# Branch outputs of the hybrid mixer: chunks in pairs on TensorE, six block sums on GpSimd

## The reference, cut to what matters

```
g = sigmoid(gates.reshape(b, s, 3, 1024))
merged = g[:, :, 0] * (o_fox @ w_fox_out) + g[:, :, 1] * (o_dsa @ w_dsa_out) + g[:, :, 2] * (o_sb @ w_sb_out)
return merged @ w_out
```

## Time and profile before

| what | value |
|---|---|
| runs | 2165.32, 2165.68, 2166.57 us; median 2165.68 |
| the profiled execution | 2165.68 us, its span 2163.6 us (2.1 us lie around the span) |
| TensorE busy | 2153.1 us of the span |
| VectorE, ScalarE, GpSimd busy | 1507.8, 597.0, 459.0 us |
| branch stage, first layer | 420.46 to 451.28 us from the span's start |
| branch stage, second layer | 1156.53 to 1187.34 us |

### The profile page before, as it was taken

The page is one execution under the profiler, slowest core; times in us unless marked ns, Lnnn a source line. Parts: engine busy times, 40 slices in busy tenths (PEclk is TensorE's granted clock), DMA queues, the critical chain, the costliest instruction groups (busy, mean ns, idle before and its releaser), DMA issues.

```text
span 2163.6 us, 44071 instructions
## 1 busy us (share of the span) xinstructions
PE 2153.1 (100%) x17524; PEld 2071.0 (96%) x17524; DVE 1507.8 (70%) x3184; ACT 597.0 (28%) x1608; POOL 459.0 (21%) x652
## 2 busy tenths in 40 slices
PE   9999999999999999999999999999999999999998
PEld 8999999899999999999998999999989999889998
DVE  6774856787776677668477777665758774768775
ACT  2210233512221022004433222201425520434530
POOL 1110003600222022100153002211214431313440
PEclk9999999999999999999999999999999999999999
DMA  9556654443664566456544545555636646637653
GB/s 256 164 163 181 165 141 127 137 144 118 188 168 156 169 171 171 162 166 166 148 118 124 169 132 163 164 178 143 181 99 174 174 156 168 175 98 180 163 164 109
DMA packets 571605, 340.40 MB, mean 157 GB/s; under 512 B 45332, under 2 KB 567432, under 8 KB 571400
## 3 DMA queue, kind: packets, MB, share of 16 engines
q1 hardware_dynamic: 566736, 335.46, 55.0%
q10 hardware_dynamic: 4392, 1.08, 0.2%
q0 software_dynamic: 272, 1.05, 0.1%
HBM read 336.49 MB, written 1.05 MB: 156 GB/s over the span
## 4 chain that ended last, share of the span: by engine, by line
PE 85%; issue 8%; POOLq 3%; POOL 2%; DVE 1%; DVEq 0%; ACT 0%; ACTq 0%
PE bank L1105 40%; PE bank L1183 15%; PE bank L719 8%; PE bank L788 4%; PE bank L728 3%; PE bank L905 3%; PE bank L1381 2%; PE bank L1348 1%; PE bank L1341 1%; PE bank L1055 1%; POOLq L2308 1%; POOL arena L2310 1%; PE bank L1230 1%; PE bank L1530 1%; POOLq L2326 1%
## 5 line engine op out<-in xcount | busy, mean ns | idle before, releaser
L1105 PE MATMUL bank<-work,arena 128*128 128x128 f32 x3096 | 387.9, 275 | 0.0
L1105 PEld LDWEIGHTS bank<-work,arena 128*128 128x128 f32 x3096 | 366.4, 192 | 0.0
L2403 DVE TENSOR_TENSOR arena<-ring 128x512 f32<-128x512 f32 (+1 forms) x424 | 282.3, 706 | 93.0 <-PE bank L1183 77.7
L1183 PE MATMUL bank<-gates,arena 128*128 128x128 f32 x1584 | 216.1, 275 | 0.0
L1183 PEld LDWEIGHTS bank<-gates,arena 128*128 128x128 f32 x1584 | 196.2, 192 | 0.0
L1105 PE MATMUL bank<-hT,ring 128*128 128x128 f32 x1392 | 183.9, 275 | 0.0
L1105 PEld LDWEIGHTS bank<-hT,ring 128*128 128x128 f32 x1392 | 169.6, 192 | 0.5 <-DVE work L2403 0.2
L1105 PE MATMUL bank<-work,ring 128*128 128x128 f32 x1264 | 166.3, 275 | 0.0
L2169 POOL TENSOR_TENSOR small<-small 128x2 f32<-128x2 f32 x17 | 13.4, 789 | 707.4 <-DVE small L2400 685.1
L2403 DVE TENSOR_TENSOR arena<-arena,ring 128x512 f32<-128x512 f32 (+1 forms) x212 | 146.8, 692 | 19.6
L1737 ACT ACTIVATE hT<-xT 128x512 f32<-128x512 f32 x48 | 30.1, 629 | 466.2 <-DVE xT L2406 440.4
(11 more groups left out here) (485 smaller groups left out, 3973.0 us busy)
## 6 DMA issues: line engine op xcount, KB each, us to landing
ring<-in_ffn_w_gu SPq DMA_DIRECT2D x174, 512.0 KB, 5.2
ring<-in_w_in SPq DMA_DIRECT2D x126, 512.0 KB, 5.1
ring<-in_ffn_w_down SPq DMA_DIRECT2D x112, 512.0 KB, 4.5
ring<-in_ffn_w_up SPq DMA_DIRECT2D x84, 512.0 KB, 5.3
ring<-in_w_out SPq DMA_DIRECT2D x16, 1024.0 KB, 5.1
ring<-in_ca_w_kv SPq DMA_DIRECT2D x8, 1024.0 KB, 5.2
ring<-in_ffn_w_down SPq DMA_DIRECT2D x24, 256.0 KB, 2.9
ring<-in_w_in SPq DMA_DIRECT2D x20, 256.0 KB, 4.1
```

Of the source, the lines that this page charges most:

```text
L1105: mm = pe.matmul(out_, a[:, c, :], b_[:, c, :], start=(start and c == 0), stop=(c == 3), skip_group_check=True)
L1183: mm = pe.matmul(bank[4 * half + where_][:, S * part + P * m:S * part + P * (m + 1)], stat[name][:, k, P * m:P * (m + 1)], moving, start=( ...
L2403: return v.tensor_tensor(out_, a, b, op)
```

## The change

TensorE takes the chunks in tiles (0, 1), (2, 3), (4, 5), (6), (7): the fox products of the tile's chunks, their dsa and sb products over 128 rows, then all of the tile's products over 64 rows. VectorE gates the fox banks of a tile first (into `a4` rows 0 and 3), then dsa and sb and the adds chunk by chunk. The block sums of chunks 0 to 5 move to GpSimd, which does them in a new function ahead of `memory_sums`. VectorE waits for all six of them before t2 of chunk 6; TensorE waits for four before s1 t1 and for all six before s2 t2.

```diff
+        POOL_TURNS = 6
+        BRANCH_TILES = ((0, 1), (2, 3), (4, 5), (6,), (7,))
...
-                for m in range(C):
-                    if m % 2 == 0:
+                for ms_ in BRANCH_TILES:
+                    if ms_[0] % 2 == 0:
                         view, loaded = slots.next(10)
...
+                    for m in ms_:
+                        b = free("proj_done")
+                        for k in range(3):
+                            mm = pe.matmul(b[:, 0:S], view[:, m % 2, k, :], oT[:, k, :], start=(k == 0), stop=(k == 2))
+                        mm.then_inc(sem["proj_done"], 1)
+                    if ms_[0] == 0:
                         pe.wait_ge(sem["dve_released"], outputs_kept)
...
+                    half_rows = []
+                    for m in ms_:
+                        for own, p0 in (((3, 4), 0), ((5, 6), HD)):
+                            b = free("proj_done")
+                            for k in own:
+                                pe.matmul(b[:, 0:S], view[:, m % 2, k, :], oT[:, k, :], start=(k == own[0]), stop=False)
+                            half_rows.append((b, m, p0))
+                    for b, m, p0 in half_rows:
+                        pe.matmul(b[:, 0:S], view[p0:p0 + HD, m % 2, 7, :], oT[p0:p0 + HD, 7, :], start=False, stop=True)\
                           .then_inc(sem["proj_done"], 1)
...
+                        if q == 0 and out_ is rc and snap == 0:
+                            pe.wait_ge(sem["chunk_turned"], turned - 2)
+                        if q == 0 and snap == 1:
+                            pe.wait_ge(sem["chunk_turned"], turned)
...
+            def branches_turned():
+
+                for m in range(POOL_TURNS):
+                    pool.wait_ge(sem["chunk_merged"], n("chunk_merged"))
+                    t1, t2, t3, t4 = (t_[:, m % 4, :] for t_ in merged_t)
+                    if m < 4:
+                        pool.tensor_tensor(t1, hsT[:, m, P:S], hsT[:, m, 0:P], ALU.subtract)\
+                            .then_inc(sem["chunk_turned"], 1)
+                        continue
+                    pool.drain()
+                    pool.tensor_tensor(t2, hsT[:, m, P:S], t1, ALU.subtract)
+                    pool.tensor_tensor(t3, hsT[:, m, P:S], hsT[:, m - 4, P:S], ALU.subtract)
+                    pool.drain()
+                    pool.tensor_tensor(t4, hsT[:, m, 0:P], t2, ALU.subtract).then_inc(sem["chunk_turned"], 1)
...
+                branches_turned()
                 memory_sums()
...
+                def merge(m, fox):
+                    v.drain()
+                    tt(a4[:, 1, :], fox, a4[:, 1, :], ALU.add)
+                    v.drain()
+                    tt(hsT[:, m, :], a4[:, 1, :], a4[:, 2, :], ALU.add).then_inc(sem["operand_ready"], 1)
+                    if m < POOL_TURNS:
+                        v.drain().then_inc(sem["chunk_merged"], 1)
                     else:
+                        v.drain()
+                        if m == POOL_TURNS:
+                            v.wait_ge(sem["chunk_turned"], n("chunk_turned", POOL_TURNS))
...
                     if m in (2, 4):
                         make_sums()
+
+                def gated(k, m, dst):
+                    v.wait_ge(sem["proj_done"], n("proj_done"))
+                    tt(dst, gates[:, C * k + m, :], seen("dve", "proj_done")[:, 0:S], ALU.mult)\
+                        .then_inc(sem["dve_released"], 1)
+
+                for ms_ in BRANCH_TILES:
+                    for m in ms_:
+                        gated(0, m, (a4[:, 0, :], a4[:, 3, :])[m - ms_[0]])
+                    for m in ms_:
+                        for k in (1, 2):
+                            gated(k, m, a4[:, k, :])
+                        merge(m, (a4[:, 0, :], a4[:, 3, :])[m - ms_[0]])
```

More of the change, by code:

```diff
@@ L347, in build @@
                "pair_turned", "pair_sums", "pair_done", "pair_copied", "pair_added", "z_ready", "hidden_made",
-               "pairs_kept", "scores_kept", "gate_turned", "gate_sums", "gate_paired", "gate_kept", "gate_kept_v", "gate_added",
+               "chunk_merged", "chunk_turned", "pairs_kept", "scores_kept", "gate_turned", "gate_sums", "gate_paired", "gate_kept", "gate_kept_v", "gate_added",
                "gates_ready",
@@ L1337, in attention1 @@
                         pe.wait_ge(*loaded)
[L1338 to L1343, removed]
-                        pe.wait_ge(sem["dve_released"], outputs_kept)
[L1345 to L1350, removed]
+                    for m in ms_:
[4 more added lines that the diff above has]
+                    if ms_[0] == 0:
+                        pe.wait_ge(sem["dve_released"], outputs_kept)
+                    half_rows = []
[7 more added lines that the diff above has]
+                        pe.matmul(b[:, 0:S], view[p0:p0 + HD, m % 2, 7, :], oT[p0:p0 + HD, 7, :], start=False, stop=True)\
                           .then_inc(sem["proj_done"], 1)
@@ L1356, in attention1 @@
                 branches_read = banks.released()
+                turned = n("chunk_turned", POOL_TURNS)
                 for q in range(4):
@@ L3084, in mixer1 @@
                 v.wait_ge(sem["gates_ready"], n("gates_ready"))
[L3085 to L3089, removed]
+                def merge(m, fox):
                     v.drain()
-                    tt(a4[:, 0, :], a4[:, 0, :], a4[:, 1, :], ALU.add)
+                    tt(a4[:, 1, :], fox, a4[:, 1, :], ALU.add)
                     v.drain()
[L3093 to L3097, removed]
-                    else:
+                    tt(hsT[:, m, :], a4[:, 1, :], a4[:, 2, :], ALU.add).then_inc(sem["operand_ready"], 1)
+                    if m < POOL_TURNS:
+                        v.drain().then_inc(sem["chunk_merged"], 1)
+                    else:
+                        v.drain()
+                        if m == POOL_TURNS:
+                            v.wait_ge(sem["chunk_turned"], n("chunk_turned", POOL_TURNS))
+                        t1, t2, t3, t4 = (t_[:, m % 4, :] for t_ in merged_t)
                         ins = tt(t2, hsT[:, m, P:S], t1, ALU.subtract)
```

## The result

Six runs of the changed kernel have a median of 2173.9 us (2173.4 to 2177.1), six of the kernel before on the same chip 2166.1: a ratio of 1.0039, 95% interval 1.0029 to 1.005, so 7.8 us slower. The profiled execution took 2173.69 us, its span is 2171.5 (before: 2163.6).

A forecast was written before the change was run, and what follows sets the result against it. TensorE was taken as the bound, 0.06 us ahead of VectorE. Per layer 0.35 (chain) + 3.0 (`memory_sums` collision) + 0.6 (chunk sums) = 3.95 us; two layers 7.9, so 2165.7 + 7.9 = 2173.6 us, range 2165.8 to 2178.6.

The forecast's parts named there:

- The bound and its margin: Branch stage: TensorE bounds the kernel, with a margin of 0.06 us over VectorE at t2 of chunk 7.
- The switch: TensorE's branch stage: five stretches of half-height work instead of eight save 1.2 us a layer, 2.4 in all.
- rival (c): t2 of chunk 7 comes early enough that TensorE keeps its 1.2 us a layer: 2163.3 us, chance 0.04.
- VectorE's chain: VectorE from chunk 4 to t2 of chunk 7, without GpSimd in its way: t2 ends 0.35 us later a layer.
- I take 0.6: GpSimd's chunk sums collide with VectorE's `make_sums`: 0.6 us a layer, least 0, most 1.4.
- the term of 0.35: Delay of t2 of chunk 7 a layer, GpSimd aside; bounds 1.2 us gained to 0.35 + 0.6 lost.
- that cover: GpSimd's sums of chunks 0 to 3 precede VectorE's wait for a pair, so cost nothing; without it 4 x 0.46.
- The collision: `memory_sums`, from about 450.5, holds up VectorE's sums of chunks 6 and 7: 3.0 us a layer, 1.5 to 5.1.
- The claim on the wait later: Cross-attention asks for `memory_sums` more than 20 us after GpSimd's list ends, so that wait stays at nothing.
- Rival (a): TensorE's clock falls to 1.2 GHz around its waits, 2.3 us a fall: 2175.9 or 2178.2 us, chance 0.33.
- (b): GpSimd's turns fall between VectorE's sums, only the order of work costs: 2166.4 us, up to 2169; chance 0.18.
- (d): TensorE's half-height products don't run as one stretch, saving nothing there; forecast unchanged, no chance given.

The follow-up runs named there:

- memory_first: The changed kernel with `memory_sums` put back ahead of the chunk sums in GpSimd's list: 2168.50 us, beside 2165.40 for the kernel before.
- deferred_later: Changed kernel, `memory_sums` ahead of chunk sums, VectorE's second `make_sums` behind chunk 7 and behind the first `w_out` pair's residual: 2163.51 us, beside 2165.41 before.
- before_held: The kernel before with one added wait: GpSimd starts `memory_sums` only when VectorE has done chunk 5; 2173.27 us beside 2165.76.
- sums_alone: The changed kernel with chunks one at a time as before, GpSimd's chunk sums still ahead of `memory_sums`: 2174.26 us, beside 2165.40 for the kernel before.
- deferred: The changed kernel with `memory_sums` ahead of the chunk sums and VectorE's second `make_sums` moved from behind chunk 4 to behind chunk 7: 2164.54 us, beside 2165.76 before.
- pairs_alone: The changed kernel with TensorE's pairs only: VectorE makes all block sums, `memory_sums` in its earlier place; 2170.53 us, beside 2165.40 for the kernel before.
- memory_last: The changed kernel with `memory_sums` waiting until VectorE has done chunk 7: 2174.24 us, beside 2165.40 for the kernel before.

## Why the prediction was right

**Result.** 2173.6 us forecast, 2173.9 measured, slower by over 0.2%. Step by step:

**The bound and its margin** held. With 0.06 us between t2 of chunk 7 and its product, what delays t2 shows in the time: in memory_first 2 x 1.43 = 2.9 us of t2 point, 2168.50 - 2165.40 = 3.1 us of time.

**The switch** was right: 1.20 us a layer, and it shows in the time only when t2 comes early enough (deferred_later), as rival (c) had it for the change itself.

**VectorE's chain** was right in kind, short in size. I said 0.35 + 0.6 = 0.95 us a layer; memory_first shows 34.66 - 33.23 = 1.43. Its t2 of chunk 7 starts at 454.72 where my chain without collisions had 453.7, 1.02 later. Of this, 0.70 is collisions: the second `make_sums` 0.46 (3.22 us from 444.22 to 447.44 instead of 2.76), and the first add of chunk 6, beside chunk 5's sums on GpSimd, 0.24 (0.66 for 0.42). So "I take 0.6" was short by 0.1 only. The other 0.32 is what the term of 0.35 left out. Some 0.15 is idle time behind the merges of chunks 4 and 5: 0.20 us ahead of `make_sums` and 0.13 ahead of chunk 6's gatings, where my 1.85 holds 0.09 each, the step from the second add to t1 in the earlier trace rows. (The drain there is not new; it now carries an increment, and the next instruction behind it is another.) Another 0.15 is that the last two of the four gatings at 441.59 start near 442.25, where I had 442.1. I had put the sums of chunks 0 to 3 at nothing, since a wait for a pair would come behind them. But VectorE's last such wait is at 434.73, and chunk 2's sum, on GpSimd from 436.62, comes after it: the first two sums of the first `make_sums` take 1.53 us beside it instead of 1.29. The step that failed is "I take +0.35, since it rests on rows throughout", with that cover in it.

**The collision** was right: 3.0 said, 2.72 measured (after against memory_first), 2.9 in before_held. `memory_sums` began at 450.59 (said: 450.5) and ended at 456.33. It hit chunk 6's last add, t2 and t4, three turns of 0.9 us; I had "three or four" and priced a turn at up to 1.27. Chunk 7's first add, which began 0.18 us before its end, took 0.46 for 0.42; the second add and t2, which I had on the list too, came behind it. Of the range of 1.5 to 5.1, the row nearest in kind gave the value. The Trainium skill's rule ("SBUF — State Buffer", "SBUF: two separate sides") says that the first comer holds the ports for its whole instruction. The rows agree for VectorE: its add with two SBUF inputs ends just behind GpSimd's sum, and gatings with one input in a bank don't wait. They add that GpSimd pays too: its first three sums took 1.44, 1.45 and 1.33 for 1.27.

**The claim on the wait later** ("asks for `memory_sums` more than 20 us later") held in every kernel: no wait of TensorE for GpSimd.

**Rival (a)**: the mechanism came, its price did not. The clock was at 0.50 for 3.4 us in each layer, in the first from 452.05 on, 2.2 us into the wait for chunk 6. I had priced a fall at 2.3 us; in the profiled execution it cost nothing. The slow products (2.04 and 1.61 us) lie between two waits, and the second, for t2 of chunk 7, ends when VectorE says: slow products only shorten TensorE's idle time. In sums_alone the same 3.4 us fall behind the last wait and cost 1.6 and 1.4 us. My 2.3 was half of 4.6 us at the kernel's start, which I had read as the lower level from the pace of its MATMULs alone; the view's granted clock there is 1.00, so no row shows that fall, and those of the runs are shorter. Whether a fall cost time in other runs of the changed kernel is not shown: those of 2175.8 and 2177.1 us have a mean granted clock of 0.997 and 0.996 (0.998 in the profiled one), and no trace. I had looked for a fall in the right place and had not asked what ends last behind it.

**Rivals (b), (c) and (d)**: none came. (b) was told apart by three turns of three that went to GpSimd, (c) by t2 at 457.21, (d) by eight MATMULs in one stretch.

The sum is 4.15 us a layer at the t2 point (37.38 - 33.23) against 3.95: two errors of +0.5 and -0.3, which partly cancel. Two such layers would be 8.3 us, and the medians differ by 7.8: that the forecast came within 0.3 us is in part luck, though direction and place rest on the runs.

## What to carry to other kernels

Before work is put ahead of something on an engine that has time, look at what stands behind it in that engine's list, and at what it will then run beside: `memory_sums` was late for nobody, and cost 5 us by its place alone. A saving on the bounding engine reaches the end only if the chain behind it, here VectorE's, is shortened by as much; what stands in that chain and is needed later can be moved, and then what stands behind its new place has to be checked (in deferred the residual came late, in deferred_later nothing did). In these traces a fall of the clock cost nothing where a later wait for another engine followed, and 1.4 to 1.6 us where none did.

## What the runs showed that I had not expected

**The clock's falls don't follow the length of the wait alone.** In the changed kernel it fell 2.2 us into a wait of 2.55 in the first layer, and in the second 0.1 us after work had come back from one of 2.56; in sums_alone it fell 1.1 us after work had come back from a wait of 2.13. In before_held the same wait of 2.59 us brought a fall in the second layer and none in the first, and in pairs_alone a wait of 2.4 brought none in either. In memory_last it fell in the second layer, 0.7 us behind a wait of 1.66, and not in the first. Busy time by stretch of pairs_alone, across its waits in the second layer, and then of memory_last, its fall:

```profile
1187.00:1191.00 4.00, 1.60 (x12) 1.06 (x11) 3.50 (x13) 0.00 (x0) 0.00 (x0) 1.00 0.41 136
1191.00:1195.00 4.00, 3.22 (x29) 3.03 (x28) 3.67 (x11) 0.83 (x3) 0.00 (x0) 1.00 0.36 126
```

```profile
1192.40:1195.80 3.40, 3.40 (x19) 3.40 (x18) 2.86 (x10) 0.55 (x2) 0.18 (x1) 0.50 0.66 232
```

Each of these falls lasted 3.4 us. What decides on one stays open; no run was made for it. The kernels with a long wait here are less even than the others, and the clock goes along with it: of the ten runs of pairs_alone, those of 2169.1 and 2169.3 us have a mean granted clock of 0.999, those of 2171.1 and 2171.6 one of 0.997.

**A short GpSimd sum costs VectorE less than a long one.** A VectorE add that meets a 128x128 sum of GpSimd (0.46 us) lost 0.24 us, one that meets a 128x512 sum (1.27 us) lost 0.9. By these two the loss grows with the length of the other engine's instruction; whether the same memory sums in shorter pieces would cost less was not tried.
